# State-space x, B and C projections by block products in a stage of their own

## What is computed

```python
h = rmsnorm(x, mix_norm_w[layer])
proj = h @ w_in                                   # 1024 x (2048 z, 2048 x, 512 B, 512 C, 32 dt)
xbc = silu(causal_depthwise_conv(proj[x, B, C], conv_w, conv_b))    # 4 taps along the tokens
dt = softplus(proj[dt] + dt_bias)
y = ssd_chunked(x, dt, A, B, C) + x * D           # 4 groups, 8 chunks of 128 tokens each
y = grouped_rmsnorm(y * silu(z)) * norm_w
x = x + y @ w_out
```

## Time and profile before

| | us |
|---|---|
| median of the runs | 2308.45 |
| lowest and highest run | 2308.16 and 2309.12 |
| span of the profiled execution | 2307.1 |

### The profile page before, as it was taken

How to read it: one execution, slowest core, us unless ns; L and a number is a source line. 1 busy time by engine, 2 the same in 40 slices (tenths; PEclk the granted TensorE clock), 3 DMA queues, 4 the chain that set the end, 5 groups by cost and what they waited for, 6 DMA issues and landing times.

```text
span 2307.1 us, 29399 instructions
## 1 busy us (share of the span) xinstructions
PE 2286.2 (99%) x10830; PEld 1870.6 (81%) x10830; DVE 1261.0 (55%) x1660; ACT 1056.0 (46%) x1901; POOL 1197.2 (52%) x842
## 2 busy tenths in 40 slices
PE   8999999999999999999999999999999999999998
PEld 6877878888888888788888888888878888888887
DVE  7356663333336777557258247338763333336777
ACT  4046543333333446475256247238543333333445
POOL 3224288777774654223224223314388777774654
PEclk9999999999999999999999999999999999999999
DMA  5100322323228743121222212113222323227754
GB/s 162 48 26 19 119 87 87 119 87 123 88 106 295 243 149 112 57 92 47 65 61 68 73 41 88 49 52 101 101 81 94 119 87 119 87 101 282 256 148 158
DMA packets 166964, 247.92 MB, mean 107 GB/s; under 512 B 18464, under 2 KB 111532, under 8 KB 164268
## 3 DMA queue, kind: packets, MB, share of 16 engines
q1 hardware_dynamic: 162204, 233.99, 30.7%
q10 hardware_dynamic: 4624, 12.06, 1.4%
HBM read 192.93 MB, written 53.08 MB: 107 GB/s over the span
## 4 chain that ended last, share of the span: by engine, by line
PE 93%; DVE 2%; POOL 2%; issue 1%; DMA 1%; ACT 1%; SPq 0%; ACTq 0%; POOLq 0%; DVEq 0%
PE ps L1752 32%; PE ps L1478 12%; PE ps L1480 12%; PE ps L1479 12%; PE ps L1838 5%; PE ps L1846 5%; PE ps L1842 5%; PE ps L2038 1%; PE ps L2030 1%; POOL p_lo L774 1%; PE ps L2023 1%; POOL p_val L800 1%; PE ps L1501 1%; PE ps L1675 1%; PE ps L1708 1%
## 5 line engine op out<-in xcount | busy, mean ns | idle before, releaser
L749 POOL TENSOR_TENSOR w_lo<-w_raw,w_hi 128x1024 fp32r<-128x1024 f32 x74 | 176.5, 2389 | 376.3 <-ACT w_hi L927 329.7
L853 POOL TENSOR_TENSOR s_lo<-s_val,s_hi 128x512 fp32r<-128x512 f32 x154 | 234.3, 1523 | 202.3 <-ACT s_hi L1256 202.2
L2314 DVE TENSOR_TENSOR xres<-ps,xres 128x512 f32<-128x512 f32 x132 | 90.5, 688 | 409.5 <-PE ps L1752 409.5
L1478 PE MATMUL ps<-xn_hi,w_hi 128*128 128x512 f32 x784 | 310.2, 396 | 0.0
L1479 PE MATMUL ps<-xn_lo,w_hi 128*128 128x512 f32 x784 | 305.5, 390 | 0.0
L1480 PE MATMUL ps<-xn_hi,w_lo 128*128 128x512 f32 x784 | 305.3, 389 | 0.0
L774 POOL TENSOR_TENSOR p_lo<-p_val,p_hi 128x512 fp32r<-128x512 f32 x176 | 238.4, 1363 | 44.8 <-ACT p_hi L1068 33.7
L1068 ACT ACTIVATE p_hi<-p_val 128x512 fp32r<-128x512 f32 x176 | 111.1, 632 | 310.6 <-POOL p_val L800 310.6
L1752 PE MATMUL ps<-xn_hi,p_hi 128*128 128x512 f32 x704 | 189.0, 390 | 3.1 <-ACT xres L1171 3.1
L1752 PE MATMUL ps<-xn_lo,p_hi 128*128 128x512 f32 x704 | 188.2, 389 | 0.0
L1752 PE MATMUL ps<-xn_hi,p_lo 128*128 128x512 f32 x704 | 188.2, 389 | 0.0
(11 more groups left out here) (293 smaller groups left out, 4922.8 us busy)
## 6 DMA issues: line engine op xcount, KB each, us to landing
s_val<-hidden SPq DMA_DIRECT2D x154, 256.0 KB, 2.8
hidden<-xres SPq DMA_DIRECT2D x20, 1792.0 KB, 6.5
wv_g<-in_w_gate SPq DMA_DIRECT2D x22, 1024.0 KB, 5.1
wv_u<-in_w_up SPq DMA_DIRECT2D x20, 1024.0 KB, 5.1
w_raw<-in_ssd_w_in SPq DMA_DIRECT2D x40, 512.0 KB, 3.9
d_val<-in_w_down SPq DMA_DIRECT2D x70, 256.0 KB, 3.9
rows_v<-in_w_down SPq DMA_DIRECT2D x64, 256.0 KB, 3.7
mdec<-decay_sums SPq DMA_DIRECT2D x32, 512.0 KB, 4.0
```

What stands on the lines that cost most here:

```text
L749: pool.tensor_tensor(w_lo[piece.slot][:, :], raw[piece.raw][:, :], f(w_hi[piece.slot][:, :]), ALU.subtract).then_inc(lo_done, 1)
L853: pool.tensor_tensor(s_lo[i][:, :], s_val[i][:, :], f(s_hi[i][:, :]), ALU.subtract)\
L1478: pe.matmul(dst, l_hi, r_hi, start=first, stop=False, skip_group_check=reopened)
```

## The change

A new stage (`q_stage` on every engine) stands between FFN 0 and the scans. Group 0's B and C are projected there plainly (`bc_sums`, 96 matmuls); the other 22 blocks form 11 pairs: x0,x1 and x2,x3 of group 0, then B,C and the two x pairs of each later group. Each pair is one gate-like ("g") or up-like ("u") half of one of six rounds p = 0 to 5 (round 5 has only "g") and takes seven products, 84 matmuls instead of 96. The product operands on the token side need sums of tokens' halves, T1 to T4, made while the last four tiles are transposed (`turn_T`, `turn_sums`, `turn_rests`, `turn_hi`, `turn_lo`). Each block of a pair ends as a row of 1024 in two banks; tap 0 (`tap0`), the taps (`taps`) and the silu (`row_silu`) work in a row buffer in `xres`, whose x is stored to DRAM (`parked_x`) before and loaded back in group 0's scan. SP stores each row to `conv_rows` in DRAM and loads a group's six rows in two halves of the tokens ahead of its scan. dt's projection moves into the last round, `step_sizes` around the last products. The groups are unrolled, the scans read their constants from `gconst` and no copy of it, and z pieces are split at other places. Places of the down slices' ring move to make room for B's and C's weights, which are loaded and split during the down slices.

The diff, cut to what is named:

```diff
@@ ring places
 RING = 5
-ring_at = [("w", 6 * DM), ("w", 3 * DM), ("s", 5 * S), ("s", 0), ("s", 2 * S), ("w", 0)]
+ring_at = [("w", 6 * DM), ("w", 10 * DM), ("w", 3 * DM), ("s", 0), ("s", 2 * S), ("w", 0)]

 def place(s):
-    return RING if s == 2 else s % RING
+    return RING if s == 1 else s % RING

@@ pieces and fillers of the scans
-HI_AFTER_CHUNK = {0: (9,), 1: (10,), 3: (11,), 4: (12,), 6: (13,)}
-LO_AFTER_MASKS = {1: (9,), 2: (10,), 3: (11,), 4: (12,), 6: (13,)}
+Z_PIECES, OUT_PIECES = range(BG), range(BG, 2 * BG)
+HI_AFTER_CHUNK = {0: (1, 2), 1: (3,), 2: (4,), 3: (5,), 4: (6,), 6: (7,)}
+LO_AFTER_MASKS = {0: (2,), 1: (3,), 2: (4,), 3: (5,), 4: (6,), 6: (7,)}
+Z_BEFORE = {False: (0, 1, 2, 3), True: (2, 3, 4)}
+Z_AFTER_CHUNK = {False: {0: (4,), 1: (5, 6), 2: (7,), 3: (8, 9), 4: (10, 11), 5: (12,), 6: (13,), 7: (14, 15)},
+                 True: {0: (5,), 1: (6,), 2: (7,), 3: (8, 9), 4: (10, 11), 5: (12,), 6: (13,), 7: (14, 15)}}
+DECAY_AFTER_PIECE = {3: (2,), 4: (3,), 5: (4,), 6: (5,), 7: (6, 7)}
@@ Sync queue
+            if layer == 0 and s in (30, 31):
+                i = s - 30
+                cols = ssd_w_in[0][:, (bc_, cc_)[i] * P:((bc_, cc_)[i] + 1) * P].rearrange("(k p) c -> p k c", p=P)
+                sp.dma_start(bc_raw[i][:, :, :], cols).then_inc(bc_loaded[i], 16)
+            if layer == 0 and s == 55:
+                sp.wait_ge(bc_lo_done, 2)
+                load_q(0, "g")
...
+    def load_rows(g, half):
+        cols = slice(half * BANK, (half + 1) * BANK)
+        bc_src = conv_rows[g * NCB:g * NCB + 2].rearrange("r p s -> p r s")
+        x_src = conv_rows[g * NCB + 2:(g + 1) * NCB].rearrange("r p s -> p r s")
+        sp.dma_start(bc_rows[:, :, cols], bc_src[:, :, cols]).then_inc(rows_loaded[half], 16)
+        sp.dma_start(yx[:, :, cols], x_src[:, :, cols]).then_inc(rows_loaded[half], 16)
...
+        sp.wait_ge(down_full, down_count(0, 6, 6))
+        load_q(0, "u")
+        for tt in range(4):
+            sp.wait_ge(down_added, add_order.count(0, "M7", tt, 0, 1))
+            sp.dma_start(parked_x[tt], xres[:, tt, :]).then_inc(x_parked[0], 16)
+        for tt in range(4, NT):
+            sp.wait_ge(down_added, add_order.count(0, "M3", tt - 4, 4, 1))
+            sp.dma_start(parked_x[tt], xres[:, tt, :]).then_inc(x_parked[1], 16)
+        store_row(0)
+        store_row(1)
+        for p in range(NQ - 1):
+            sp.wait_ge(q_lo_done, q_lo_order.count(0, p, "M4g"))
+            load_q(p + 1, "g")
+            store_row(row_at(p, "g", 1))
+            store_row(row_at(p, "g", 2))
+            sp.wait_ge(q_lo_done, q_lo_order.count(0, p, "M4u"))
+            if p + 1 < NQ - 1:
+                load_q(p + 1, "u")
+            else:
+                sp.dma_start(wdt[:, :, :], w_in[:, dtc:dtc + SH].rearrange("(k p) c -> p k c", p=P))\
+                    .then_inc(wdt_loaded, 16)
+            store_row(row_at(p, "u", 1))
+            store_row(row_at(p, "u", 2))
+
...
+        if g == 0:
+            sp.wait_ge(q_lo_done, q_lo_order.count(0, NQ - 1, "M4g"))
+            load_piece(0)
+            load_piece(1)
+            load_rows(0, 1)
+            sp.wait_ge(q_full, q_order.count(0, NQ - 1, "M4g"))
+            sp.wait_ge(sums_stored, 16)
+            load_decay(0)
+            load_decay(1)
+            load_piece(2)
+            load_piece(1)
+            sp.wait_ge(ydiag_full, t.count("chunk", -1))
+            load_decay(0)
+            sp.wait_ge(out_full, t.count("out", -NT))
+            load_rows(g, 0)
+            sp.wait_ge(out_full, t.count("out"))
+            load_decay(1)
+            load_rows(g, 1)
...
+            if g == 0 and k == 5:
+                store_row(row_at(NQ - 1, "g", 1))
+                store_row(row_at(NQ - 1, "g", 2))
+                sp.wait_ge(gc_ready, 1)
+                for i in range(4):
+                    sp.wait_ge(row_stored[i], 16 * ((len(ROWS) - 1 - i) // 4 + 1))
+                for tt in range(NT):
+                    sp.dma_start(xres[:, tt, :], parked_x[tt]).then_inc(x_back, 16)
@@ ScalarE
+    def tap0(i):
+        if i < 2:
+            act.wait_ge(bc_full, i + 1)
+        else:
+            p, m, blk = (i - 2) // 4, "gu"[(i - 2) // 2 % 2], (i - 2) % 2 + 1
+            if blk == 1:
+                act.wait_ge(q_c_ready, q_c_order.count(0, p, "12" + m))
+            else:
+                act.wait_ge(q_full, q_order.count(0, p, "M4" + m))
+        if i < 4:
+            act.wait_ge(x_parked[1], 16 * 4)
+        else:
+            act.wait_ge(row_stored[i % 4], 16 * (i // 4))
+        tap = GC_TAP + k * CONV + CONV - 1
+        act.activation(row_buffer(i), flat(row_banks(i)), ACT.Identity, scale=gconst[:, g, tap:tap + 1],
+                       bias=gconst[:, g, GC_BIAS + k:GC_BIAS + k + 1]).then_inc(tap0_done, 1)
+
+    def row_silu(i):
+        act.wait_ge(taps_done, i + 1)
+        act.activation(row_buffer(i), row_buffer(i), ACT.Silu).then_inc(row_done, 1)
...
+                act.wait_ge(q_pool_done, q_pool_order.count(0, "T4", i))
+            else:
+                act.wait_ge(q_val_ready, q_val_order.count(0, n, i))
+            turn_split(act.activation(dst, src, ACT.Copy), n, i)
+
...
+        turn_first(0)
+        act.wait_ge(x_parked[0], 16 * 4)
+        turn_hi("T1", 0)
...
+        turn_hi("T1", 1)
+        turn_hi("T2", 1)
...
+        turn_hi("T1", 2)
+        turn_hi("T2", 2)
+        turn_first(3)
+        turn_hi("T1", 3)
+        turn_hi("T2", 3)
...
+            q_copy(p, "M6g")
+            q_hi_of(p, "M6u")
+            tap0(row_at(p, "g", 1))
...
+            q_copy(p, "M1u")
+            q_hi_of(p + 1, "M1g")
+            row_silu(row_at(p, "g", 1))
+            tap0(row_at(p, "g", 2))
+            q_hi_of(p, "M4u")
+            q_hi_of(p + 1, "M2g")
+            row_silu(row_at(p, "g", 2))
+            q_copy(p, "M5u")
+            q_hi_of(p + 1, "M5g")
...
+            if (g, c) == (0, 1):
+                row_silu(row_at(NQ - 1, "g", 1))
+                row_silu(row_at(NQ - 1, "g", 2))
@@ TensorE
+    def q_stage():
+        pe.wait_ge(bc_lo_done, 2)
+        pe.wait_ge(nt_split, NT // 2)
+        pe.wait_ge(down_added, add_order.count(0, "M3", 0, 4, 1))
+        bc_sums(0, 0, 0)
+        turn_T(0)
+        bc_sums(0, 0, 1, range(4))
+        turn_T(1)
+        bc_sums(0, 0, 1, range(4, NK))
+        bc_sums(0, 0, 2)
+        pe.wait_ge(down_added, add_order.count(0, "M3", 2, 4, 1))
+        bc_sums(1, 0, 0)
+        turn_T(2)
+        bc_sums(1, 0, 1)
+        bc_sums(1, 0, 2)
+        turn_T(3)
+        pe.wait_ge(down_added, add_order.count(0, "M3", 3, 4, 1))
+        pe.wait_ge(q_turn_hi, q_turn_hi_order.count(0, "B22", 3))
+        bc_sums(0, 1, 0)
+        bc_sums(0, 1, 1)
+        pe.wait_ge(q_turn_lo, q_turn_lo_order.count(0, "B22", 3))
+        bc_sums(0, 1, 2).then_inc(bc_full, 1)
+        bc_sums(1, 1, 2).then_inc(bc_full, 1)
+        for mn in Q_FIRST:
+            q_product(0, mn)
+        for p in range(1, NQ - 1):
+            q_product(p, "M1g")
+            q_product(p - 1, "M4u")
...
+            q_product(p, "M7u")
+        p = NQ - 1
+        q_product(p, "M1g")
+        q_product(p - 1, "M4u")
+        q_product(p, "M2g")
+        q_product(p, "M5g")
+        q_product(p, "M6g")
+        pe.wait_ge(wdt_split, 3)
+        pe.wait_ge(taps_done, row_at(p - 1, "u", 2) + 1)
+        dt_rows(0)
...
+        q_product(p, "M3g")
+        folds()
+        q_product(p, "M7g")
...
+        if g == 0:
+            pe.wait_ge(taps_done, row_at(NQ - 2, "u", 1) + 1)
+            z_half(0)
+            q_product(NQ - 1, "M4g")
+            z_half(1)
+            decay_sum_rows()
+            pe.wait_ge(taps_done, row_at(NQ - 1, "g", 1) + 1)
+            token_major(0)
+            pe.wait_ge(taps_done, row_at(NQ - 1, "g", 2) + 1)
+            for i in Z_BEFORE[True]:
+                z_half(i)
@@ VectorE
+        def turn_sums(i):
+            lo_k, hi_k, c1, c2 = views(i)
+            dve.wait_ge(q_turn_hi, q_turn_hi_order.count(0, "B22", i))
+            dve.wait_ge(x_parked[0], 16 * 4)
+            value(dve.tensor_tensor(t1_new[:, :, c1], lo_k, comb_val[:, :, c1], ALU.subtract), "T1", i)
+            dve.wait_ge(q_val_ready, q_val_order.count(0, "T1", i))
+            value(dve.tensor_tensor(comb_val[:, :, c1], hi_k, t1_new[:, :, c1], ALU.subtract), "T2", i)
...
+        def turn_rests(i):
+            lo_k, hi_k, c1, c2 = views(i)
+            dve.wait_ge(q_turn_hi, q_turn_hi_order.count(0, "B22", i))
...
+        turn_sums(0)
+        turn_rests(0)
+        last_norm()
+        turn_sums(1)
+        turn_rests(1)
+        turn_rests(2)
+        turn_sums(2)
+        turn_rests(3)
+        turn_sums(3)
+        taps(0)
+        taps(1)
...
+            taps(row_at(p - 1, "u", 2))
+            q_block(p, "11", "g")
+            q_block(p, "12", "g")
+            q_block(p, "22", "g")
+            taps(row_at(p, "g", 1))
+            taps(row_at(p, "g", 2))
...
+        p = NQ - 1
```

(11 more changed lines are left out.)

978 lines of the change are left out of this document (651 added, 327 removed).

## The result

| | median us | against before, with 95% interval |
|---|---|---|
| before | 2308.78 | |
| changed | 2346.45 (2344.84 to 2347.78) | 1.0162 [1.0147, 1.0176] |

The changed kernel is slower by 38 us. The forecast was 2296.4 with a range of 2284 to 2309, so it failed, in sign too. The profiled execution has a span of 2346.0 us, 38.9 more than before.

The account below looks back on a forecast made before the run. TensorE, busy 99% of the span, was taken as the bound. From a span of 2307.1 us, -30.0 + 8 + 0.3 + 6.0 + 2.7 + 1 = -12.0 gave span 2295.1 and time 2296.4 us, range 2284 to 2309.

Parts of the forecast that it names:

- The price of a matmul: On TensorE, each matmul of 512 columns costs 0.2268 us, read from the chain of the kernel before.
- The removed matmuls: Eleven pairs at 84 instead of 96 matmuls: 132 fewer, -30.0 us.
- start of the stage: New TensorE waits for tile 4's norm, tile 7's hi part, the second product and late rests: together +8 us.
- rounds 1 to 4: Pairs run without gaps, the tight taps-and-copy chain fits under three products and loads are hidden: +0.3 us.
- end of the stage: In round 5 TensorE waits for x2's taps, +1.3, and x3's taps, +4.7: together +6.0 us.
- first scan: In group 0's scan, chunk 2's mask late by 1.0 and chunk 5's decays by 1.7 behind x's loads: +2.7 us.
- other: Boundaries of groups 1 to 3 mostly covered, down slices' ring and B and C splits in idle time: +1 us.
- clock: Rival: the clock falls in the waits of 4.4 and 4.7 us, costing +3 to +6 us; 15%.
- tile 7's hi part: At the stage's start, TensorE waits for this end of a ScalarE and VectorE chain: +4.0 us.
- (d): At the stage's start, the second round's M1g and late VectorE rests T2 to T4 beside GpSimd: +1.6 us.
- the slower rival: The chain M4, tap 0, taps, silu, copy, M3 overruns in every half pair, up to 2318 us; 8%.
- the DMA rival: x's way back, row stores and row loads exposed in first scan and at three boundaries: 2303 to 2312 us; 12%.

Follow-up runs that it names:

- a_pad1184: Changed kernel with 1184 unused bytes per partition ahead of the shared buffers, putting them at their old address 179840; 2321.6 us.
- a_pad160: Changed kernel with 160 unused bytes per partition ahead of the shared buffers; 2321.5 us.
- f3_turn: f2_xback with tile 7's three parts moved ahead of tile 6's sums on ScalarE; 2303.9 us.
- f2_xback: a_pad1184 with the next up weights' load ahead of a row's store, and x's eight loads moved to the end of the first group's list; 2308.1 us.
- a_pad416: Changed kernel with 416 unused bytes per partition ahead of the shared buffers; 2320.0 us.
- a_shift128: Changed kernel with 128 unused bytes ahead of all its buffers and 160 more ahead of the shared ones; 2315.7 us.
- b_pad32: Kernel before the change with 32 unused bytes per partition ahead of its shared buffers; 2329.7 us.
- f6_bcload: f3_turn with taps reordered at the stage's end, and B's and C's weight loads at down slices 34 and 37, not 30 and 31; 2298.7 us.

## Why the prediction was wrong, point by point

**The price of a matmul.** The step that failed is the first: a price of 0.2268 us, read from the kernel before, was used for all matmuls of the changed one, and the line of the change that drops `gc` was taken for free. The sum had no term for what a moved address does. It was 30 us by the trace and 25 by the runs (a_pad1184, a_pad160), half of the 50 us between forecast and result, and no rival had it. With the buffers at their old distance 2321.6 was left: still 25 above the forecast.

**The removed matmuls** were right: 132, and the pace of the pairs at 227 ns.

The other terms, against the trace of a_pad1184, where the price is that of before. Three of its waits:

```profile
PE ps L2522 <- POOL xds L1150: 4.6, 1, 4.6
PE ps L2318 <- ACT xn_hi L1636: 4.6, 1, 4.6
...
PE ps L2551 <- POOL sq L1166: 1.6, 3, 0.5
```

The measured values are distances between starts less the normal distance, summed by place:

| term of the sum | forecast | measured | |
|---|---|---|---|
| start of the stage | 8 | 7.7 | 0.9 and 0.7 for transposes, 4.6 for tile 7, 1.5 for taps |
| rounds 1 to 4 | 0.3 | 4.0 | the up weights' load in the second round, 3.6 |
| end of the stage | 6.0 | 6.5 | 2.8 and 3.7 |
| first scan | 2.7 | 4.7 | x's way back ahead of output weights |
| other | 1 | 7 | down slices 2, group norms 2.1, third group 1.5, FFN 1's first load 1.6 |
| clock | 0 | 10 | five falls: 3.1, 1.6, 2.2, 1.6, and 1.7 at FFN 1's start |

They sum to 40, and its span of 2318.2 is 41 above 2307.1 - 30.0.

**Start and end of the stage** were right in their main waits, place and cause: tile 7's hi part (4.6, forecast 4.0), the second product (1.5, forecast 1.4) and the last rows' taps. The chain between ScalarE and VectorE is borne out by f3_turn, which took 2.8 of the 4.6 away. That the totals agree so well is partly luck. The 1.6 of (d) did not come: six of the eleven rests took 1.2 to 1.8 us, each beside a GpSimd instruction, and five 0.68, but TensorE waited for none. In its place stand 0.7 for transposes of tiles 5 and 7 and 0.6 more at tile 7. At the end the first row's taps cost 2.8 and not 1.3, and the second's 3.7 and not 4.7.

**Rounds 1 to 4.** The tight chain of taps and copies, the slower rival's, held with its slack: no round but the second has a wait of more than 0.2 us there. What failed is the sentence on loads: "hidden" was worked out from bytes and rate, and not from the queue, where a load stood behind a store that waits for a silu.

**First scan.** The mechanism (eight loads ahead on one queue) was right, its victim and size wrong: 4.7 us, and by f2_xback 8.5 with the clock. The output weights' split stands on GpSimd ahead of a chunk's `xds`, which the step had left out.

**Clock.** It was given as a rival with 15% and 3 to 6 us for two falls. It belonged in the sum: the sum itself forecast waits of 4.4 and 4.7 us, and every wait of that length in the changed kernel's trace, from tile 7 on, has the clock at half behind it. In a_pad1184 these two falls cost 3.1 and 2.2 us, as the rival had them. The unforeseen waits brought the others, some 5 us.

**Ahead of the stage.** The two loads in the down slices were costed at nothing, with idle ScalarE and GpSimd named as cover, and the queue left out; they cost about 2 us.

**The rest.** 2.1 us at the group norms (three waits for `sq` on GpSimd) and 1.5 in the third group's last chunk (mostly a wait for its mask) had no term, and no run was made for them, so their cause is open. Chunk 0 of groups 1 to 3 waits for nothing in a_pad1184: the rows' loads, the DMA rival's three boundaries, were hidden.

## What to carry to other kernels

When an edit adds or drops a buffer, compare the start addresses of everything behind it and look at the pace of instructions that were not edited: in this kernel 32 bytes moved an untouched program by 20 us, more than twice what any of the other edits here gave, and 1184 bytes of padding gave the changed one 25 back. A load is hidden only if nothing ahead of it on its queue waits, and a split of weights that aren't due must not stand ahead of an operand that is. Where the bound engine is given a wait of some 4 us, put the return from half clock into the sum, or fill the wait.

## What the runs showed of the hardware that was not expected

- In these kernels a 512-column fp32 matmul starts 227 ns after the one before if moving and stationary operands start at the same place within 256 bytes of a partition, and mostly 231 to 235 ns after it at distances of 32, 64, 96 and 128; two places 256 apart modulo 512 are fast. Three (at 128 bytes) to eight (at 96) matmuls behind a slow product are slow too, even where their own operands lie at the same place.
- With the granted clock at 0.50 a 512-column matmul takes 427 ns. In these traces every wait of 4.2 us or more from tile 7 on had it behind it, but shorter waits of one size had it in some executions and not in others: 3.0 us at FFN 0's start in a_pad416 and not in a_shift128, 3.0 us at FFN 1's start in f2_xback and not in a_pad416. In the second round 3.6 us cost 1.6 us of clock in a_pad1184, and 3.4 us nothing in a_shift128.
- The load of 1 MB of FFN weights behind which TensorE waits at FFN 1's start took 5.15 us in the kernel before and 6.6 in the changed one, with waits of 1.5 and 2.7 us. Over all runs the waits at the FFNs' starts are 0.9 us (b_pad32) to 3.2 (f6_bcload). Some of the spread between runs of one kernel comes from there.
